# Sample convolution taps as products and sums, and the memory keys and values placed behind the input products

## The reference, cut to what matters

```python
def conv_branch(u_ext, w_dw, b_dw, g_ln, b_ln, w_out):      # u_ext: (n, 30 + t, 512)
    c = lax.conv_general_dilated(u_ext, w_dw[:, None, :], window_strides=(1,), padding='VALID',
                                 dimension_numbers=('NWC', 'WIO', 'NWC'), feature_group_count=D_CONV)
    c = jax.nn.silu(layernorm(c + b_dw, g_ln, b_ln))
    return c @ w_out

def mem_kv(mem, g, w):                                      # mem: (1, 256, 1024), w: (1024, 1024)
    mk, mv = jnp.split(rmsnorm(mem, g) @ w, 2, axis=-1)     # both are outputs, too
    ...
```

## Time and profile before

| | us |
|---|---|
| three timed runs | 2474.91, 2472.23, 2477.0 |
| their median | 2474.91 |
| span of the profiled execution | 2476.7 |
| first products, from the first tap to the end of the block | 458.8 to 587.7 |
| second products | 587.7 to 967.9 |
| next block's first instruction | 969.9 |

### The profile page before, as it was taken

How to read it: one execution, slowest core, us unless ns; L and a number is a source line. 1 busy time by engine, 2 the same in 40 slices (tenths; PEclk the granted TensorE clock), 3 DMA queues, 4 the chain that set the end, 5 groups by cost and what they waited for, 6 DMA issues and landing times. The chain is left out here.

```text
span 2476.7 us, 37131 instructions
## 1 busy us (share of the span) xinstructions
PE 2217.1 (90%) x14090; PEld 2032.2 (82%) x14090; DVE 1367.6 (55%) x2222; ACT 595.3 (24%) x1065; POOL 809.9 (33%) x591
## 2 busy tenths in 40 slices
PE   5969999997899966666778799899999999999997
PEld 5929888787899955555455699898999999999997
DVE  5078999999889993965686445333211211121123
ACT  4162222231142200321333312222211211111112
POOL 5103432311211212575765324342322322322321
PEclk9989999998999977875899899999999999999999
DMA  5003222332232225687874444311111111111112
GB/s 187 18 22 78 60 61 73 98 115 85 78 107 87 90 95 205 200 284 236 267 229 142 146 136 134 127 56 34 43 43 51 42 41 53 43 38 47 43 34 97
DMA packets 231678, 249.10 MB, mean 101 GB/s; under 512 B 37283, under 2 KB 192976, under 8 KB 228989
## 3 DMA queue, kind: packets, MB, share of 16 engines
q1 hardware_dynamic: 184974, 129.15, 17.4%
q0 software_dynamic: 23552, 70.28, 9.2%
q10 hardware_dynamic: 23031, 48.07, 5.3%
HBM read 212.37 MB, written 35.43 MB: 100 GB/s over the span
## 5 line engine op out<-in xcount | busy, mean ns | idle before, releaser
L412 POOL TENSOR_TENSOR ffn_w_lo<-ffn_w_raw,ffn_w_hi 128x1024 fp32r<-128x1024 f32 (+2 forms) x108 | 219.6, 2034 | 532.0 <-ACT ffn_w_hi L203 532.0
L390 PE MATMUL banks<-h_hi,in_w_hi 128*128 128x384 f32 (+1 forms) x1056 | 350.2, 332 | 20.3 <-PEq L1237 13.1
L392 PE MATMUL banks<-h_hi,in_w_lo 128*128 128x384 f32 (+1 forms) x1056 | 346.3, 328 | 0.0
L391 PE MATMUL banks<-h_lo,in_w_hi 128*128 128x384 f32 (+1 forms) x1056 | 346.0, 328 | 0.0
L390 PE MATMUL banks<-ffn_in_hi,ffn_w_hi 128*128 128x384 f32 (+1 forms) x1032 | 338.4, 328 | 5.3 <-POOL ffn_w_lo L412 3.8
L391 PE MATMUL banks<-ffn_in_lo,ffn_w_hi 128*128 128x384 f32 (+1 forms) x1032 | 338.1, 328 | 0.0
L392 PE MATMUL banks<-ffn_in_hi,ffn_w_lo 128*128 128x384 f32 (+1 forms) x1032 | 338.1, 328 | 0.0
L390 PE MATMUL banks<-halves,ffn_w_hi 128*128 128x384 f32 (+1 forms) x846 | 277.9, 328 | 18.6 <-DVE halves L2385 11.2
L392 PE MATMUL banks<-halves,ffn_w_lo 128*128 128x384 f32 (+1 forms) x846 | 277.7, 328 | 0.0
L391 PE MATMUL banks<-halves,ffn_w_hi 128*128 128x384 f32 (+1 forms) x846 | 277.4, 328 | 0.0
L412 POOL TENSOR_TENSOR in_w_lo<-in_w_raw,in_w_hi 128x1024 fp32r<-128x1024 f32 x48 | 130.5, 2721 | 400.7 <-ACT in_w_hi L203 400.6
(11 more groups left out here) (367 smaller groups left out, 4005.2 us busy)
## 6 DMA issues: line engine op xcount, KB each, us to landing
in_w_raw<-in_w_in SPq DMA_DIRECT2D x48, 512.0 KB, 3.8
ffn_w_raw<-in_w_ffn_in SPq DMA_DIRECT2D x44, 512.0 KB, 3.7
merge_gate<-gate_spill_dram SPq DMA_DIRECT2D x24, 544.0 KB
ffn_w_raw<-in_w_ffn_out SPq DMA_DIRECT2D x24, 384.0 KB, 3.4
gate_spill_dram<-second_out ACTq DMA_DIRECT2D x16, 544.0 KB, 2.7
room<-q_spill_dram ACTq DMA_DIRECT2D x8, 1024.0 KB, 6.9
q_spread<-q_spill_dram ACTq DMA_DIRECT2D x8, 1024.0 KB, 6.8
gate_spill_dram<-first_out ACTq DMA_DIRECT2D x8, 544.0 KB, 2.8
```

The source lines that it names most:

```text
L390: nc.tensor.matmul(out, self.w_hi[:, s, k, :], g.hi[:, k, a:a + w], start=(k == 0), stop=False)
L391: nc.tensor.matmul(out, self.w_hi[:, s, k, :], g.lo[:, k, a:a + w], start=False, stop=False)
L392: mm = nc.tensor.matmul(out, self.w_lo[:, s, k, :], g.hi[:, k, a:a + w], start=False, stop=(k == g.kc - 1))
L412: self.m.nc.gpsimd.tensor_tensor(self.w_lo[:, s, 0:g.kc, :], self.raw[:, s, 0:g.kc, :], self.w_hi[:, s, 0:g.kc, :], ALU.subtract).then_inc ...
```

## The change

The wide taps: chunks 0, 1 and 2 are all done in the first stage, in turn; chunk 3 alone remains for the second. The narrow taps go: for each of the 8 sample positions one product of all 4 chunks, 8 sequences and 31 taps (992 elements a partition, into the room of `smask`) and one sum over the taps; then four additions of the bias.

The memory keys and values: PE transposes the memory rows in two halves ahead of the memory queries and ahead of the own queries; ACT evacuates them, and the result goes over the memory rows themselves. The product follows the last unit at once, ahead of the list's transposes, and ACT alone evacuates it and its transposes back. The mirroring of the list goes between the transposes back. Five weight slots take the place of four, the first a tile of its own, and the order of the slots is changed. SP issues all weight groups ahead of the wait for `s_listed`. The stores of keys and values are no longer awaited in this stage; the one place that overwrites the tile, a stage later, waits for them.

```diff
-HALF_TAPS = 16
+FIRST_CHUNKS = 3
...
@@ conv_taps
             if k > k0:
-                dve.wait_ge(tap, 2 * ((k - 1 - k0) * len(chunks) + i + 1))
-            for dst, src in ((m.cT[:, c, 0:SEQ], m.u[:, c, k:k + SEQ]),
-                             (m.cT[:, c, SEQ:NT].rearrange("p (s t) -> p s t", s=NSEQ), m.us[:, c, :, k:k + TDEC])):
...
+                dve.wait_ge(tap, (k - 1 - k0) * len(chunks) + i + 1)
+            dst, src = m.cT[:, c, 0:SEQ], m.u[:, c, k:k + SEQ]
...
+def sample_taps(nc, m, dve, products, windowed, summed):
...
+    window = products.rearrange("p (c s k) -> p c s k", c=KC, s=NSEQ)
+    taps = m.wdw[:, :, :].unsqueeze(2).to_broadcast([P, KC, NSEQ, CW])
+    dst = m.cT[:, :, SEQ:NT].rearrange("p c (s t) -> p c s t", s=NSEQ)
+    for t in range(TDEC):
+        if t:
+            dve.wait_ge(summed, t)
+        nc.vector.tensor_tensor(window, m.us[:, :, :, t:t + CW], taps, ALU.mult).then_inc(windowed, 1)
+        dve.wait_ge(windowed, t + 1)
+        nc.vector.tensor_reduce(dst[:, :, :, t], window, AX, ALU.add).then_inc(summed, 1)
+    dve.wait_ge(summed, TDEC)
+    for c in range(KC):
+        nc.vector.tensor_scalar(m.cT[:, c, SEQ:NT], m.cT[:, c, SEQ:NT], m.bdw_sb[:, c:c + 1], None, ALU.add
+                                ).then_inc(summed, 1)
...
@@ stage_first_products, vector
-                conv_taps(nc, m, dve, early_tap, range(2))
-                conv_taps(nc, m, dve, half_tap, (2,), 0, HALF_TAPS)
+                conv_taps(nc, m, dve, early_tap, range(FIRST_CHUNKS))
...
@@ stage_second_products, sync
+                for c in range(KD):
+                    if c in (1, 2):
+                        sp.wait_ge(gemm.lo_done, 2 * gemm.first[-1] + c)
+                    elif c in (3, 4):
+                        sp.wait_ge(gate_out[c - 3], 16 * (NR + 1))
+                    elif c > 4:
+                        sp.wait_ge(kv_full, c - NSLAB + 1)
+                    sp.dma_start(slabs[c % NSLAB], wcols(m.w_mem_kv, c * P, P)).then_inc(kv_w_in[c % NSLAB], 16)
+                sp.wait_ge(s_listed, 1)
...
-                sp.wait_ge(stored, 32)
...
@@ tensor
-                pe.wait_ge(half_tap, 2 * (CW - HALF_TAPS))
-                pe.wait_ge(late_tap, 2 * CW)
+                pe.wait_ge(late_tap, CW * (KC - FIRST_CHUNKS))
+                pe.wait_ge(s_sample, TDEC + KC)
...
+                memory_turned(0)
                 gemm.tensor_segment(pe, 5)
-
+                memory_turned(2)
                 gemm.tensor_segment(pe, 6)
...
+                pe.wait_ge(mem_ev, 4)
+                for c in range(KD):
+                    pe.wait_ge(kv_w_in[c % NSLAB], 16 * (c // NSLAB + 1))
+                    if c >= 2:
+                        pe.wait_ge(kv_ev, c - 1)
+                    for k in range(KD):
+                        mm = nc.tensor.matmul(m.B[6 + c % 2][:, 0:NMEM].rearrange("p (t n) -> p t n", t=2),
+                                              slabs[c % NSLAB][:, k, :], memT[:, k, :, :],
+                                              start=(k == 0), stop=(k == KD - 1))
+                    mm.then_inc(kv_full, 1)
                 pe.wait_ge(s_listed, 1)
...
+                    if n == 1:
+                        pe.wait_ge(s_copied, 1)
+                        for f in range(2):
+                            mm = nc.tensor.matmul(m.B[1][:, f * NS:(f + 1) * NS], m.mirror[:, :],
...
@@ scalar
                 for i, evac in ((1, evac_memory_queries), (2, evac_own_queries)):
+                    for n in (2 * i - 2, 2 * i - 1):
+                        act.wait_ge(mem_turned, n + 1)
+                        for k in range(4):
+                            c = 4 * (n % 2) + k
+                            cp = nc.scalar.activation(memx[:, n // 2, c * P:(c + 1) * P],
+                                                      m.B[6 + n % 2][:, k * P:(k + 1) * P], ACT.Identity,
+                                                      scale=m.g_mem_sb[:, c:c + 1])
+                        cp.then_inc(mem_ev, 1)
...
-                for c in range(0, KD, 2):
+                for c in range(KD):
...
+                for n in range(4):
+                    act.wait_ge(kv_t, n + 1)
+                    nc.scalar.copy(mkv[:, n // 2, (n % 2) * 512:(n % 2) * 512 + 512], m.B[6 + n % 2][:, :]
+                                   ).then_inc(kv_t_ev, 1)
...
@@ vector
-                conv_taps(nc, m, dve, half_tap, (2,), HALF_TAPS, CW)
-                conv_taps(nc, m, dve, late_tap, (3,))
+                conv_taps(nc, m, dve, late_tap, range(FIRST_CHUNKS, KC))
+                sample_taps(nc, m, dve, m.smask[:, 0:2 * KC * NSEQ * CW].bitcast(F32), s_window, s_sample)
```

More of the change, by code:

```diff
@@ L1105, in conv_taps @@
             if k > k0:
[L1106 to L1115 removed]
+                dve.wait_ge(tap, (k - 1 - k0) * len(chunks) + i + 1)
+            dst, src = m.cT[:, c, 0:SEQ], m.u[:, c, k:k + SEQ]
+            if k == 0:
+                nc.vector.tensor_scalar(dst, src, m.wdw[:, c, 0:1], m.bdw_sb[:, c:c + 1],
+                                        ALU.mult, ALU.add).then_inc(tap, 1)
+            else:
+                nc.vector.scalar_tensor_tensor(out=dst, in0=src, scalar=m.wdw[:, c, k:k + 1], in1=dst,
+                                               op0=ALU.mult, op1=ALU.add).then_inc(tap, 1)
+    dve.wait_ge(tap, (k1 - k0) * len(chunks))
+def sample_taps(nc, m, dve, products, windowed, summed):
[12 more added lines that the diff above has]
+                                ).then_inc(summed, 1)
+    dve.wait_ge(summed, TDEC + KC)
 class NarrowGemm(StepGemm):
@@ L1783, in stage_second_products @@
             "squared", "inverted", "rooted", "chain", "done"))
[L1784 to L1788, removed]
+        NSLAB = 5
+        slabs = [ctx.enter_context(nc.sbuf_tensor("memkv_w", [P, KD, P], F32))[:, :, :], gemm.raw[:, 0], gemm.raw[:, 1],
+                 gate[:, 0, 0:KD * P].rearrange("p (k n) -> p k n", k=KD),
+                 gate[:, 1, 0:KD * P].rearrange("p (k n) -> p k n", k=KD)]
+        kv_w_in = [m.sem(f"memkv_w_in{i}") for i in range(NSLAB)]
+        kv_full, kv_ev = m.sem("memkv_full"), m.sem("memkv_evac")
+        kv_t, kv_t_ev = m.sem("mkv_turned"), m.sem("mkv_evac")
         with nc.Block() as block:
@@ L1799, in _ @@
                     gemm.load_weights(sp, u)
[L1800 to L1814, removed]
+                for c in range(KD):
[7 more added lines that the diff above has]
+                sp.wait_ge(s_listed, 1)
+                sp.wait_ge(s_coded, 1)
+                for s in range(2):
+                    sp.wait_ge(gate_out[s], 16 * (NR + 1))
+                sp.dma_start(m.omT[:, :, :], m.queries_spill[:, 0:MH, :]).then_inc(q_back, 16)
+                sp.dma_start(m.qT[:, :, :], m.queries_spill[:, MH:, :]).then_inc(q_back, 16)
                 sp.wait_ge(kv_t_ev, 4)
-                sp.dma_start(m.o_mk.rearrange("(t p) n -> p t n", p=P), mkv[:, :, 0:512]).then_inc(stored, 16)
-                sp.dma_start(m.o_mv.rearrange("(t p) n -> p t n", p=P), mkv[:, :, 512:1024]).then_inc(stored, 16)
-                sp.wait_ge(stored, 32)
+                sp.dma_start(m.o_mk.rearrange("(t p) n -> p t n", p=P), mkv[:, :, 0:512]).then_inc(m.mkv_stored, 16)
+                sp.dma_start(m.o_mv.rearrange("(t p) n -> p t n", p=P), mkv[:, :, 512:1024]).then_inc(m.mkv_stored, 16)
                 sp.wait_ge(s_pages, 16 * 16)
@@ L1867, in _ @@
                 mm.then_inc(s_rows, 1)
[L1868 to L1883, removed]
+                pe.wait_ge(kv_ev, KD)
                 for n in range(4):
```

50 lines of the change are left out of this document (22 added, 28 removed).

## The result

The changed kernel takes 2527.39 us, the median of four runs (2512.52 to 2528.8), against 2475.28 for the kernel before, measured beside it: a ratio of 1.0199, 95% interval 1.0177 to 1.022. It is 52 us slower where 41 us faster was forecast, and no rival in the prediction gives this time for its reason.

A forecast was written before the change was run, and what follows sets the result against it. PE's waits for DVE (taps, mean, list) and the serial tail were taken as the bound; 9.2 from taps, 27.9 from overlap and tail and 3.8 from stores make 40.9 off the 2474.91 median: 2434.0 us, range 2425 to 2448.

The forecast's parts named there:

- The step that failed: First product stage: narrow taps saved and 15 wide ones added cancel, 126.7 before, 127.8 after; block ends 1.0 later.
- the 2.2: DVE time that one POOL subtraction costs beside the taps, read as 2.1 to 2.2 a time.
- more gained: Rival, first stage: wide taps aren't stalled by POOL, block ends up to 11 us earlier, 2423 to 2427; chance 0.06.
- the slower rival: Rival, second stage: strided products and sums run at a fraction of the rate, 4.68 each, 2489; chance 0.03.
- PE's 13.1 at the border: Border of the two product stages: PE's 13.1 us wait for DVE, read as a wait for taps.
- Taps of the second stage: Second stage: taps done 2.9 us before PE asks, so PE's wait ahead of the mean goes, 7.5 us.
- the 2.7 of the clock: Mean's products: without the wait PE stays at full clock, 7.6 us in place of 10.2, 2.7 less.
- the some 2 us named in the prediction: Second stage: by the skill's rule the new sums spare DVE some 2 us of POOL stall, total the same.
- Memory part: End of second block: products overlap the wait for the list, 27.9 us from overlap and tail, 3.8 from stores.
- the gather stage: Length carried over unchanged at 460 us; rival that it gives some gain back, 2437 to 2447, chance 0.11.
- own bounds: Margin on the forecast total from first stage, clock, tail and stalls: 2428 to 2442 us.
- the 0.13 that the prediction took from the rows: DVE taps: waiting for the op just before costs 0.13, from pairs at 1.52 against 1.39.

The follow-up runs named there:

- one wait a round: Changed kernel, but each round of three wide first-stage taps waits once, for the whole round before it; 2439.38 us, ratio 0.9854.
- a fill of 8 columns: Changed kernel plus one unused 8-column fill on DVE behind each round of three wide taps, no added wait; 2437.37 us, ratio 0.985.
- a stop only every 34 us: Changed kernel, but only at every eighth round does the first wide tap wait for the whole round before; 2445.07 us, ratio 0.9882.
- two chunks in turn: Changed kernel, but the first stage runs chunks 0 and 1 in turn, then chunk 2 alone, each tap behind the one before; 2490.53 us, ratio 1.004.
- 128 or 256 columns: Changed kernel plus one unused two-input product-and-sum of that width behind each round of three wide taps; 2537.51 us (128) and 2541.95 us (256).

## Why the prediction was wrong, point by point

**The step that failed** is the first stage: "93 wide at 1.20, less 1.4, and again 8 x 2.2 … the block ends 1.0 later". It prices what POOL costs DVE, and takes from the kernel before that POOL gets in eight times. It never asks where POOL gets in. All 14 subtractions of the earlier trace rows got in at the border from a wide tap to a narrow one; the row at 651.94, which the prediction used for the 2.2, shows just that: the narrow tap ends with the subtraction. The first one beside the taps, and the narrow tap that it held up (0.28 otherwise):

```profile
467.24 2.64 POOL L412 TENSOR_TENSOR in_w_lo<-in_w_raw,in_w_hi 128x1024 fp32r<-128x1024 f32 x1 [4.02 <-ACT in_w_hi L203]
```

```profile
467.48 2.48 DVE L1113 SCALAR_TENSOR_TENSOR room<-room,w_dw 128x64 f32<-128x64 f32 x1
```

No two wide taps stood side by side in that kernel, so its trace could not show what a row of them does to POOL. The change deletes the narrow taps. POOL then waits 101 us, the weights' low parts come that late, and PE, which the prediction held to be "done long before", is 91.1 late. The rival "more gained" held the clue ("All stalled taps in the trace are narrow ones") but asked from the wrong side, whether wide taps are stalled by POOL; the slower rival lay in the sums, which were fine. Broken by a stop in each round, the chain behaves nearly as priced: eight subtractions, each holding up one wide tap to 3.3 or 3.4 us, and 130.3 us from the first tap to the last (455.36 to 585.64), against 127.8 and some 3.5 for thirty stops.

**A second reading in that step was wrong, without effect on the time.** PE's 13.1 at the border was put down to taps. In the changed kernel DVE is done at 658.2, 20 us ahead of the border, and PE still waits 13.0. The first instruction of POOL behind the border says who was last:

```profile
678.75 0.24 POOL L1845 IOTA sel_within<- 128x128 f32 x1 [8.21 <-POOLq L1258]
```

POOL's own sequencer ends 8.21 us of idle time there, and the kernel before has the same 8.20. With one wait a round, where DVE's taps end later than that, DVE is the last: it idles 0.5 there and POOL 10.5. So in the kernel before the 13 us behind PE's last product are POOL's. DVE had 1.8 us in hand there: taps that end earlier would have brought nothing, not the up to 11 of "more gained", and taps that end 1.0 later would not have counted in full.

**Taps of the second stage: right.** They are done at 747.54, PE asks at 752.37: 4.8 ahead, forecast 2.9. PE's wait for them is gone, and the clock at the mean is 1.00 (the window 753 to 762 above), so the 2.7 of the clock came too: the mean's products take 7.55 in place of 10.14. A product and a sum take 1.19 each and start 1.22 apart, forecast 1.22. Rows of DVE and one of POOL:

```profile
742.09 1.19 DVE L1132 TENSOR_REDUCE room<-smask 128x32 f32<-128x992 f32 x1
743.31 2.23 DVE L1130 TENSOR_TENSOR smask<-room,w_dw 128x992 f32<-128x992 f32 x1
```

```profile
742.10 2.40 POOL L412 TENSOR_TENSOR in_w_lo<-in_w_raw,in_w_hi 128x1024 fp32r<-128x1024 f32 x1 [8.44 <-ACT in_w_hi L203]
```

The sum runs its 1.19 beside POOL's subtraction, the product behind it is held up; it is the same at the subtraction before (730.24). The Trainium skill (SBUF — State Buffer, section Who interferes with whom) says that a reduction never contends; these two sums agree, where the trace of before had none to show it. The two subtractions cost DVE 0.9 and 1.0 in place of 2.2 each, the some 2 us named in the prediction.

**Memory part: right.** Less 91.1 for the late border, the last unit ends at 891.3 (forecast 893.5), the list at 913.2 (914.0), the products at 918.9 (921.1), 27.6 behind their start (forecast 27.6). The last store is issued by 923.6 (927.0), but the read of the queries ends the block at 927.2, not the 925 that was forecast for it. The 10.2 of the earlier trace rows is the middle of two reads; the later one, which counts, took 12.6 before and takes 13.5 now. The second block is 40.6 shorter, forecast 41.9. Behind it the time is unchanged, so the gather stage gave nothing back. With the chain of taps broken, the profiled span is 2435.4, against 2476.7 - 40.9 = 2435.8 by the sum. That agreement is in part luck: the profiled run (2437.01) is the fastest of its four, and the time of a run is 1.6 above its span wherever both are known, so that the profiled run of before was one of about 2478.3, 3.4 above its median. In medians it is 35.5 less (2474.91 to 2439.38), with runs of before from 2471.49 to 2484.46.

**Slips in the sums, without effect.** The own bounds add up to 11.6 on the upper side, 2446 and not 2442. The bound of the rival "slower" adds the 2.7 of the clock where the sentence ahead of it takes it off: with it taken off, 3.8 an instruction in place of 4.0, and 1.19 was measured.

## What to carry to other kernels

Before a short instruction between long ones is removed from DVE, look in the trace for what starts at it: an engine that shares a port may live on that border. Price contention from both sides, what the other engine costs this one and what this one costs the other, and follow the second to whoever waits for it. A single stop of 0.04 us every few instructions, or a fill of 8 columns, is enough to let POOL in; with a stop only every 34 us PE waits again, 6.3 us here.

## What was not expected of the hardware

**A chain holds the shared port, not an instruction.** The Trainium skill (SBUF — State Buffer, section SBUF: two separate sides) says that of a DVE instruction with two SBUF inputs and a GpSimd instruction that reads SBUF the one that starts first has the shared pair for the whole instruction, and the other is blocked. By that POOL would wait one wide tap, 1.28 us, at most (an estimate). Here it waited 101 us for a chain of wide taps that overlap by 0.08 (start to start 1.196, length 1.28), 65 us with two chunks in turn, and up to 114 us with 128 or 256 columns in between.

**What opens it is only half known.** POOL got in at the next border wherever the round had a stop of 0.04 us or a fill in it, also at borders of that round without a stop: five of the eight in the run with one wait a round have the usual overlap of 0.08. Without a stop it got in only ahead of an instruction of 64 columns (0.28 us), never at the borders around 128 (0.35 us) or 256 columns (0.48). What in the port's logic makes the difference stays open. Open, too, is why one of four runs of the changed kernel, and three of eight with two chunks in turn, are some 14 us shorter: no profile of such a run was taken.

**A wait for the instruction just before costs 0.11 to 0.12.** With one wait a round the taps without a wait start 1.196 apart and those with one 1.31. The Trainium skill (VectorE: DVE Perf Modes, section The DRAIN you can't avoid) has a semaphore behind each operation at no extra cost; here it costs 0.11 to 0.12 a time, near the 0.13 that the prediction took from the rows.
